# Even-block attentions: group ends in other steps, a larger ring, a second sum buffer, and the band mask added by TensorE

## The reference, cut to what matters

```python
def gqa_attend(q, k, v, bias=None, sink=None):
    s = jnp.einsum("bqhgd,bkhd->bhgqk", q, k) * ATTN_SCALE
    if bias is not None:
        s = s + bias
    if sink is not None:
        p = softmax(concatenate([s, sink_col], axis=-1))[..., :-1]
    else:
        p = softmax(s, axis=-1)
    return jnp.einsum("bhgqk,bkhd->bqhgd", p, v)
...
rel = jnp.arange(band)[None, :] - B_WINDOW - jnp.arange(Q_BLOCK)[:, None]
in_band = jnp.abs(rel) <= B_WINDOW
...
y_lat = jnp.concatenate([oa * silu(ag), ob * silu(bg)], axis=-1) @ w_out
```

## Time and profile before

| what | value |
|---|---|
| time, median of 3 runs | 3530.72 us (3527.99 to 3532.56) |
| the profiled execution's own time | 3532.62 us |
| its span, first to last instruction | 3530.8 us |
| attention A | 262 to 577 us |
| evB | 577 to 760 us |
| attention B | 760 to 982 us |
| evO | 982 to 1132 us |
| TensorE busy over the span | 93% |
| VectorE busy | 38% |
| ScalarE busy | 20% |
| GpSimd busy | 11% |

### The profile page before, as it was taken

The page is one execution under the profiler, slowest core; times in us unless marked ns, Lnnn a source line. Parts: engine busy times, 40 slices in busy tenths (PEclk is TensorE's granted clock), DMA queues, the critical chain, the costliest instruction groups (busy, mean ns, idle before and its releaser), DMA issues.

```text
span 3530.8 us, 27181 instructions
## 1 busy us (share of the span) xinstructions
PE 3281.2 (93%) x11342; PEld 1705.4 (48%) x11342; DVE 1340.9 (38%) x1692; ACT 710.4 (20%) x877; POOL 380.2 (11%) x244
## 2 busy tenths in 40 slices
PE   7897888987799999998999998999999999999998
PEld 4453345644455444447884533454444444444443
DVE  3727773357655169214661311034222222221001
ACT  3106551013300100014441122112001111110000
POOL 0004662004300000008220000000000000000000
PEclk9999998998899999999999999999999999999998
DMA  6000001010042101014110101000101111110011
GB/s 231 24 30 1 1 1 36 25 55 1 1 155 90 32 17 54 30 34 112 26 35 30 31 12 48 30 18 24 36 30 36 42 36 42 36 46 33 33 49 48
DMA packets 38042, 145.61 MB, mean 41 GB/s; under 512 B 4928, under 2 KB 5440, under 8 KB 35872
## 3 DMA queue, kind: packets, MB, share of 16 engines
q1 hardware_dynamic: 31680, 126.40, 10.6%
q0 software_dynamic: 6240, 17.47, 2.1%
HBM read 139.66 MB, written 6.82 MB: 41 GB/s over the span
## 4 chain that ended last, share of the span: by engine, by line
PE 85%; DVE 6%; issue 3%; ACT 3%; POOL 2%; DMA 1%; SPq 0%; DVEq 0%; ACTq 0%; POOLq 0%
PE ps L677 49%; PE ps L1151 9%; PE ps L1091 4%; PE ps L1044 3%; PE ps L810 3%; PE ps L838 3%; PE ps L973 2%; POOL x_ctx L602 2%; DVE x_ctx L1732 1%; PE ps L825 1%; PE ps L903 1%; PE ps L932 1%; PE ps L921 1%; PE ps L1068 1%; PE ps L785 1%
## 5 line engine op out<-in xcount | busy, mean ns | idle before, releaser
L677 PE MATMUL ps<-arena 128*128 128x512 f32 (+1 forms) x4192 | 1716.2, 571 | 22.8 <-ACT arena L1203 7.6
L677 PEld LDWEIGHTS ps<-arena 128*128 128x128 f32 x4192 | 799.4, 191 | 930.9 <-issue 904.6
L1151 PE MATMUL ps<-arena 128*128 128x512 f32 x704 | 302.3, 592 | 0.0
L1920 DVE SCALAR_TENSOR_TENSOR arena<-ps,vectors,arena 128x1023 f32<-128x1023 f32 x44 | 56.4, 1283 | 461.5 <-ACT arena L1416 461.5
L1151 PEld LDWEIGHTS ps<-arena 128*128 128x128 f32 x704 | 133.8, 190 | 168.4 <-issue 168.4
L903 PE MATMUL ps<-arena 64*128 64x512 f32 x504 | 156.7, 704 | 31.2 <-DVE x_ctx L1732 26.9
L1416 ACT ACTIVATE arena<-ps,vectors 128x1024 f32<-128x1024 f32 x44 | 52.9, 1203 | 537.5 <-PE ps L677 537.5
L1822 DVE SCALAR_TENSOR_TENSOR x_ctx<-arena,vectors,x_ctx 128x1024 f32<-128x1024 f32 x120 | 154.2, 1285 | 4.3
L1783 DVE TENSOR_TENSOR x_lat<-ps,x_lat 128x1024 f32<-128x1024 f32 x16 | 19.6, 1224 | 354.6 <-PE ps L1151 281.8
L1091 PE MATMUL ps<-arena 128*128 128x512 f32 x256 | 131.3, 637 | 11.7 <-ACT arena L1401 11.7
L810 PE MATMUL ps<-arena,x_ctx 128*128 128x512 f32 (+2 forms) x384 | 132.7, 430 | 8.9 <-ACT arena L1262 7.2
(11 more groups left out here) (214 smaller groups left out, 2986.5 us busy)
## 6 DMA issues: line engine op xcount, KB each, us to landing
arena<-in_wall SPq DMA_DIRECT2D x188, 512.0 KB, 3.6
arena<-expanded_bias POOLq DMA_DIRECT2D x80, 160.0 KB, 3.9
arena<-in_wdown SPq DMA_DIRECT2D x8, 1408.0 KB, 6.1
x_lat<-in_xl_in SPq DMA_DIRECT2D x4, 1024.0 KB, 9.5
x_lat<-in_xl_in SPq DMA_DIRECT2D x2, 2048.0 KB, 9.7
out<-x_lat SPq DMA_DIRECT2D x8, 512.0 KB, 3.1
expanded_bias<-in_rpb POOLq DMA_DIRECT2D x1, 2560.0 KB, 17.8
x_ctx<-in_dmask POOLq DMA_DIRECT2D x5, 320.0 KB, 3.5
```

The costliest lines, as they stand in the source:

```text
L677: mm = pe.matmul(ps[:, o + c:o + c + n], W[:, ring_of(g) % WSLOTS, k, :], rhs(k, c, n), start=(k == 0), stop=(k == KT - 1))
L1151: mm = pe.matmul(ps[:, o + c:o + c + n], WD[m % 2][:, k, :], ACTV[:, k, c:c + n], start=(k == 0), stop=(k == DOWN_K - 1))
```

## The change

- `group_plan`: B, PV, NB and what follows are one step later. The two halves of MT become M0 and M1, in two steps. DEN and MIX come one more step later than OE.
- Rings: A has 18 buffers instead of 14, B has 13 instead of 9. A buffer more is the second sum buffer; GpSimd alternates between the two by group, and waits for DEN of the group before the last.
- The mask: ScalarE copies all items. For a masked item TensorE adds the mask to the scores with a product of the identity and the mask, repeated over four heads.
- The gates: ScalarE's copy and O_EVAC go. VectorE multiplies G by PV_O (OE) and later by the reciprocals (MIX), both from PSUM. OE stands after B, F and the reductions of its step.
- In a step with NB and F, VectorE does F before B.
- SP: half the residual is no longer loaded after A. The first four weight tiles of evO are asked for before the end of B; after it x_lat and the context come in four pairs of tiles among the late weights.

```diff
 def group_plan(sizes):
-        at = max(at + 1, first[g + 1] - 1 + 2)
+        at = max(at + 1, first[g + 1] + 2)
         steps[at]["B"] = n
         steps[at + 2]["PV"] = n
         if j == 0:
-            steps[first[g + 1]]["MT"] = g
+            steps[first[g + 1]]["M0"] = g
+            steps[first[g + 1] + 1]["M1"] = g
             steps[at]["NB"] = g
         if j == sizes[g] - 1:
             steps[at + 3]["OE"] = g
-            steps[at + 3]["DEN"] = g
-            steps[at + 4]["MIX"] = g
+            steps[at + 4]["DEN"] = g
+            steps[at + 5]["MIX"] = g
...
-        RING_A = [XL[:, k, :] for k in range(KT)] + [area(SCR + 1024 * i, 1024) for i in range(6)]
-        RING_B = [XL[:, k, :] for k in range(4, KT)] + [area(SCR + 1024 * i, 1024) for i in range(5)]
+        LOW = [XL[:, k, :] for k in range(KT)] + [area(SCR + 1024 * i, 1024) for i in range(6)]
+        HIGH = [area(22016 + 4 * TOK + 1024 * i, 1024) for i in range(5)]
...
+            at = {..., "ring": ring[:-1], "sums": [PROB_SUM, ring[-1]], ...}
...
 GpSimd
+                    total = at["sums"][g % 2]
                     if j == 1:
-                        if g:
-                            pool.wait_ge(at["den"], g)
+                        if g >= 2:
+                            pool.wait_ge(at["den"], g - 1)
...
 TensorE
                             mm = pe.matmul(ps[:, o:o + BANK], QK[r, 4, kt * P:(kt + 1) * P], QK[r, 0:4, c0:c1],
-                                           start=True, stop=True)
+                                           start=True, stop=mask is None)
+                        for half in range(2 if mask is not None else 0):
+                            o = S_T + (2 * (n % 2) + half) * BANK
+                            mm = pe.matmul(ps[:, o:o + BANK], IDENT, mask.unsqueeze(1).to_broadcast([P, HEADS // 2, P]),
+                                           start=False, stop=True)
...
-                    if "MT" in st:
-                        max_transposes(st["MT"], 0)
+                    for half in range(2):
+                        if f"M{half}" in st:
+                            max_transposes(st[f"M{half}"], half)
...
 ScalarE
-                    if "OE" in st:
-                        ...
-                        act.activation(O_EVAC, ps[:, PV_O:PV_O + BANK], ACT.Copy).then_inc(at["o_out"], 1)
-                    if "F" in st and not at["is_masked"][st["F"]]:
+                    if "F" in st:
...
 VectorE
                 for st in at["plan"]:
+                    if "NB" in st and "F" in st:
+                        maximum(st["F"])
+                    if "B" in st:
+                        subtract(st["B"])
+                    if "F" in st and "NB" not in st:
+                        maximum(st["F"])
...
+                    if "OE" in st:
+                        g = st["OE"]
+                        gv = mixed_in(g)
+                        dve.wait_ge(at["pv"], first[g + 1])
+                        dve.tensor_tensor(gv, ps[:, PV_O:PV_O + BANK].rearrange("p (m q) -> p m q", m=4), gv, ALU.mult)\
+                           .then_inc(at["o_out"], 1)
...
                         dve.tensor_tensor(gv, ps[:, MISC:MISC + BANK].rearrange("p (m q) -> p m q", m=4), gv, ALU.mult)\
-                           .then_inc(at["scaled"], 1)
-                        dve.wait_ge(at["scaled"], g + 1)
-                        dve.wait_ge(at["o_out"], g + 1)
-                        dve.tensor_tensor(gv, O_EVAC.rearrange("p (m q) -> p m q", m=4), gv, ALU.mult).then_inc(at["mixed"], 1)
+                           .then_inc(at["mixed"], 1)
```

More of the change, by code:

```diff
@@ L272, in program @@
         rows_in_sbuf = sem("modulation_rows_in_sbuf")
-        x_back = [sem("residual_low_tiles_back"), sem("residual_high_tiles_and_context_back")]
+        x_back = [sem(f"residual_pair{i}_back") for i in range(KT // 2)]
         q_padded = sem("queries_padded")
@@ L409, in program @@
             for st in plan:
-                at["misc"] += [("MT", st["MT"], 0), ("MT", st["MT"], 1)] if "MT" in st else []
+                for half in range(2):
+                    at["misc"] += [("MT", st[f"M{half}"], half)] if f"M{half}" in st else []
                 at["misc"] += [("DEN", st["DEN"], 0)] if "DEN" in st else []
@@ L415, in in_ring @@
         def in_ring(at, n):
-            k = sum(at["is_masked"][:n + 1])
-            return (at["masked"], k) if at["is_masked"][n] else (at["filled"], n + 1 - k)
+            return at["filled"], n + 1
         def scores_read(at, n):
@@ L895, in soft_attention @@
                         g, j = items[n]
-                        kt = groups[g]["keys"][j][0]
+                        kt, mask = groups[g]["keys"][j]
                         c0, c1 = groups[g]["q"]
@@ L951, in _ @@
             even_half("evB", False)
+            pe.wait_ge(bmask_in, 32)
             pe.wait_ge(qk_done, 10)
@@ L1698, in soft_attention, with mixed_in, subtract @@
                 ring, groups, items, first = at["ring"], at["groups"], at["items"], at["first"]
+                def mixed_in(g):
+                    c0, c1 = groups[g]["q"]
+                    return G[:, at["g_rows"]:at["g_rows"] + 4, c0:c1]
+                def subtract(n):
+                    g, j = items[n]
+                    if j == 0:
+                        dve.wait_ge(at["bcast"], g + 1)
+                    p = ring[n % len(ring)]
+                    dve.tensor_tensor(p, ps[:, NM_BC:NM_BC + 1024], p, ALU.add).then_inc(at["shifted"], 1)
@@ new lines, in maximum @@
+                def maximum(n):
+                    g, j = items[n]
+                    if j == 0:
+                        return
+                    o = S_T + 2 * (n % 2) * BANK
+                    dve.wait_ge(*in_ring(at, n))
+                    if j == 1:
+                        dve.wait_ge(*in_ring(at, n - 1))
+                        if g:
+                            dve.wait_ge(at["max_t"], 2 * g)
+                        one = ring[(n - 1) % len(ring)]
+                    else:
+                        dve.wait_ge(at["maxed"], at["max_before"][g] + j - 1)
+                        one = KEY_MAX
+                    dve.tensor_tensor(KEY_MAX, ps[:, o:o + 2 * BANK], one, ALU.max).then_inc(at["maxed"], 1)
@@ new lines, in soft_attention @@
+                    if "F" in st and "NB" not in st:
+                        maximum(st["F"])
+                    for half in range(2):
+                        if f"M{half}" not in st:
+                            continue
+                        g = st[f"M{half}"]
+                        nm = ST[:, g % 4, 1, :]
+                        dve.wait_ge(at["max_t"], 2 * g + half + 1)
+                        dve.tensor_reduce(nm[:, 4 * half:4 * half + 4],
+                                          ps[:, MISC:MISC + BANK].rearrange("p (h k) -> p h k", h=4), AX_X, ALU.max,
+                                          negate=True).then_inc(at["reduced"], 1)
+                        if half == 0:
+                            continue
```

105 lines of the change are left out of this document (28 added, 77 removed).

## The result

The changed kernel takes 3596.98 us (median of four runs, 3591.40 to 3600.28) against 3531.64 us for the kernel before in the same session: a ratio of 1.0185, 95% interval 1.0167 to 1.0203. It is slower by 65 us, where 27 were forecast, and outside the forecast's range (3532 to 3582). The direction was right and the size was not. The profiled execution is 3591.4 us against 3532.62, +58.8, and all of it lies in the two attentions.

The account below looks back on a forecast made before the run. The prediction took the order of waits through the engines, once per query group in the two attentions, as the bound. A +9 and B +18 made +27 on 3532.62: 3560, or 3558 us as median; range 3532 to 3582.

Parts of the forecast that it names:

- The output product as the new stall: Each group: TensorE's first value product waits for VectorE's output product, standing 5.6 us.
- the maximum of the broadcast's step in front of the first subtraction: VectorE in the broadcast's step: the subtraction waits for scores, copy and maximum, starting 3.3 us later.
- The full-clock count of the group: Hand count of one group of A in the changed kernel: 33.5 us at full clock.
- The loads: Residual reloaded whole after B: hidden by about 0.5 us, up to +2 if not; earlier weight loads 0.
- The end of A: GpSimd's waits and TensorE's repeated order go, one more addition overlaps: -4 us.
- The mask was put on the path: B: mask products between scores and copy, 1.74 us an item, 3.5 per group of five, all taken as cost.
- One spell of 3.4 us costs 1.7: 35.2 us, +1.8 per group, six groups, +11.: Attention A: low clock behind the new stall lengthens each group; bounds 0 and +3.5 per group.
- B's terms: Opening +2.5, two earlier groups +1.6 and +3, four full groups +11, four-tile group +2, end -2: +18 us.
- The clock costing no more: Rival: waits move as forecast, but the clock loses no more than before; about 3534 us, chance 0.19.
- the mask hiding: Rival: VectorE's lost additions pay for the mask products; about 3542 us; chance 0.62 together with the forecast.
- The faster case: Rival: VectorE finishes the output product before TensorE needs it, removed waits count fully; -20, 3511 us, chance 0.12.
- clock low over most of each group: Rival: the low clock holds as in B now; A +20, B +30, 3581 us, chance 0.07.

Follow-up runs that it names:

- c1: Changed kernel, but VectorE takes the output product at the head of its step, before subtraction and maximum: 3537.03 us, ratio 1.0019 to the kernel before.
- c2: Changed kernel, but in the broadcast's step VectorE subtracts first and takes the maximum second: 3559.79 us, ratio 1.0084 to the kernel before.
- c3: Changed kernel with both orders: output product at the head of its step, subtraction before maximum in the broadcast's step: 3493.34 us, ratio 0.9896.
- c4: Changed kernel, but TensorE makes five unread 512-column products while it waits for the output product: 3576.81 us, ratio 1.0134 to the kernel before.
- c5: Changed kernel with the band mask of B left out of the computation: 3570.20 us, ratio 1.0115 to the kernel before.
- c10: Changed kernel with the eight 2-column denominator products replaced by one of 16 columns from head 7's sums: 3531.86 us, ratio 1.0002 to the kernel before.
- c6: Kernel before with only the larger rings, the second sum buffer and the new loads: 3508.64 us, ratio 0.9935.
- c7: c3 with the mask added by VectorE as in the kernel before: 3478.65 us, ratio 0.9855 to the kernel before.
- c8: Changed kernel with GpSimd's additions in attention B left out, sum buffers set to 1.0 once: 3580.19 us, ratio 1.0142 to the kernel before.
- c9: c7 with the kernel before's steps in `group_plan`; rings and second sum buffer stay: 3511.05 us, ratio 0.9942 to the kernel before.
- c11: c7 with the denominators cut to one 16-column product from head 7's sums: 3441.23 us, ratio 0.9733 to the kernel before.

## Why the prediction was right in direction and wrong in size

**Right.** The output product as the new stall, its length (5.58 for 5.6 us), and the maximum of the broadcast's step in front of the first subtraction. c1 and c2 remove the two causes one by one, c3 both, and the stall goes 5.58, 3.32, 3.45, 1.19. The full-clock count of the group stands: 33.5, and 33.59 in c4. ScalarE's waits for GpSimd in A, 18.6 and 12.0 us before, are 0.6 and 0.6. The loads are 0. The end of A was put at -4 and measured -5.2. The mask was put on the path, 3.5 us a group at 1.74 an item; c5 gives 1.52 an item.

**The step that failed: "One spell of 3.4 us costs 1.7: 35.2 us, +1.8 per group, six groups, +11."** The clock costs some 4.1 us per group (37.7 less 33.6), and the six intervals from the broadcast at 316.52 to that at 538.29 are 221.8 us against 201.0: +20.8 instead of +11. The spell is longer than the one counted (5.3 us from the end of the stall), and in four of six groups there is a second, of 3.4 us, behind the denominators, which no group of c10 has. What a spell costs is not half its length everywhere either: one of 3.4 us cost 0.4 us in the kernel before (33.41 for 33.04), nothing in c6, and 1.64 in c3, c4 and c7. The first two intervals gave +3.2 for the +2 forecast, so that A is 3.2 + 20.8 - 5.2 = +18.8, where +9 stood. The upper bound of that step, +3.5 per group, is what the six groups have on the mean (20.8 / 6), and the four long ones, at 4.1 to 4.4, lie over it.

**B's terms, in the main by the same cause.** Forecast and measured: opening +2.5 and +3.8; the two intervals before the full groups +1.6 and +3.4, then +3 and +11.1; four full groups +11 and +17.1; the four-tile group +2 and +2.9; the end -2 and +2.0. That sums to +40.3, for +18. The largest miss, 8 us, is the interval 816 to 848, which has a clock of 0.79 over its length and the denominators in it at half clock:

```profile
829.16 1.40 PE L924 MATMUL ps<-x_lat,arena 128*64 128x256 f32 x8 [3.95 <-DVE arena L1749]
830.49 3.58 PE L933 MATMUL ps<-consts,x_ctx 128*128 128x2 f32 x16
834.00 2.08 PE L901 MATMUL ps<-arena 64*128 64x512 f32 x4
```

The full groups are 29.6 us on the mean, for the 28.0 counted. Their clock, 0.87 over the four, means 7.7 us at the lower level in each, some 1.3 of them inside the stall. Half of the other 6.4 is 3.2 us, and 25.9 + 3.2 = 29.1 is an estimate of what the clock explains; 2.1 stood in its place. A second part that the prediction did not have is GpSimd's hold on the minimum with the sink, now that the second reduction comes while GpSimd adds; what it costs stays open (c8), with 0.46 us per group as what one group shows.

**The rivals.** The clock costing no more (3534) and the mask hiding (3542) are refuted by c4 and c5. The faster case decided at one point, the output product done by 13.2 us in the count, and it stood at 18.1. The rival "clock low over most of each group", A +20 and B +30, 3581, was nearest in size and had been given 0.07. Its A is nearly the measured +18.8, by luck: its condition did not hold, since the clock behind the stall was low for 8.7 of 37.7 us, and its B is 10 us short.

**What the parts are worth.** From c6: rings, sum buffer and loads, -22. From c6 to c9: the gates' products on VectorE, +2. From c9 to c7: the later steps, -32 with both orders right. From c7 to c3: the mask's move to TensorE, +15 with both orders right (leaving the mask out of the changed kernel gives 21 by the profiled executions, c5). From c3 to the changed kernel: the two misplaced operations, +104. These five steps are one chain from the kernel before to the changed one, and sum, unrounded, to +66, where +65 was measured. The change holds two gains, hidden behind two misplaced operations on VectorE and a mask on the path.

**Left open.** What decides whether the second spell comes. Behind a stall of 5.58 us it comes in four of six groups of A in the changed kernel and in two in c8, behind one of 3.45 in two (c2), behind one of 3.32 in none (c1). Behind a stall of at most 1.2 us a spell follows the denominators in two groups of six in c3 and c4 and in three in c7. With one 16-column product it follows them in none (c10, c11). So the short products have a part in it, and another part was varied by no run. The 7.7 us that c8 gained in A have no edit behind them, so a few microseconds of any comparison above may be the spells' own.

## What to carry to other kernels

When a bank's reader moves from one engine to another, it belongs at the head of the new engine's step, since the first writer of the next group waits for it; an operation that waits for a chain through two other engines belongs behind the one that can start at once. Cost the clock not by the spell that the kernel had but by the new stall, and look for short products within the next few microseconds, which can bring it down again. Time each part of a joint change alone: here the gain of 54 us and the loss of over 100 stood in one diff.

## What the runs showed of the hardware

- In four of six groups the clock fell a second time behind sixteen 2-column records (1.95 us); in the one shown TensorE had been busy without a gap from 401.27 on. With one product of 16 columns (0.40 us) in their place it did so in none of six (c10).
- Those sixteen records cost 1.95 us at full clock and 3.58 at half; two products of 64 x 512 outputs take 1.03.
- With a stall of 1.19 us the clock was 1.00 over four of six groups and 0.94 over two (c3); with those of 3.32 and 3.45 us (c1, c2) it was 0.90 over most groups.
- A spell of 3.4 us at 1.2 GHz cost nothing in c6 (31.0 us with and without it) and 1.64 us in c3 (30.83 for 29.19).
- An 8-column operation of VectorE with two SBUF inputs took 1.46 us in place of 0.17 under a GpSimd addition. The Trainium skill, page "SBUF — State Buffer", section "SBUF: two separate sides", says that such a pair hold a port pair against each other for a whole instruction; the trace agrees, down to the common end (877.41 and 877.38).
